# Rounding three output-projection weight chunks on GpSimd instead of ScalarE

## The reference

```python
hin = _rms_norm(x, norm_g[0])
z = hin @ w_in                                   # 1024 -> 2964, split into three head groups
y_moba = _moba_attention(...)                    # 4 heads x 64: top-3 past blocks of 256 keys + own block
y_ml = _mlstm_chunkwise(...)                     # 4 heads, qk 64, v 128, chunkwise matrix memory
y_nsa = _nsa_attention(...)                      # 4 query heads x 64: compressed + selected + window
y = concat([_head_norm(y_moba), _head_norm(y_ml) * sigmoid(lo), _head_norm(y_nsa)])
x = x + _rms_norm(y @ w_out, norm_g[1])          # the output projection, 1024 x 1024
hm = _rms_norm(x, norm_g[2])
y = square(relu(hm @ w1)) @ w2                   # MLP, hidden 4096
return x + _rms_norm(y, norm_g[3])
```

## Time and profile before

| | |
|---|---|
| time, median of 3 runs | 604.87 us (604.27 to 605.67) |
| the profiled execution | 604.64 us |
| its span in the trace | 602.9 us |
| busy in the span: TensorE | 593.0 us (98%) |
| VectorE | 387.6 us (64%) |
| ScalarE | 300.2 us (50%) |
| GpSimd | 256.5 us (43%) |
| attention in the trace | about 160 to 214 us |

### The profile page before, as it was taken

The page is one execution under the profiler, slowest core; times in us unless marked ns, Lnnn a source line. Parts: engine busy times, 40 slices in busy tenths (PEclk is TensorE's granted clock), DMA queues, the critical chain, the costliest instruction groups (busy, mean ns, idle before and its releaser), DMA issues.

```text
span 602.9 us, 8291 instructions
## 1 busy us (share of the span) xinstructions
PE 593.0 (98%) x3099; PEld 484.9 (80%) x3099; DVE 387.6 (64%) x665; ACT 300.2 (50%) x529; POOL 256.5 (43%) x137
## 2 busy tenths in 40 slices
PE   8999999999999999999999999999999999999995
PEld 5898888767867678899878888888888888888884
DVE  6414605265878773983999767585595685771657
ACT  7623414654589933555645536444345255454322
POOL 8563323573094610053357453631723626711611
PEclk9999999999999999999999999999999999999999
DMA  9743282365013820028034350621603404104002
GB/s 325 289 149 130 75 205 71 87 176 193 1 45 89 276 66 0 1 72 279 1 140 139 119 161 1 203 77 55 203 23 139 140 1 150 60 1 174 1 35 106
DMA packets 36580, 67.18 MB, mean 111 GB/s; under 512 B 2876, under 2 KB 23612, under 8 KB 35516
## 3 DMA queue, kind: packets, MB, share of 16 engines
q1 hardware_dynamic: 36236, 66.25, 34.1%
q10 hardware_dynamic: 304, 0.39, 0.3%
HBM read 62.18 MB, written 2.10 MB: 107 GB/s over the span
## 4 chain that ended last, share of the span: by engine, by line
PE 94%; ACT 2%; issue 2%; DVE 2%; POOL 0%; POOLq 0%; ACTq 0%; DVEq 0%
PE ps L1809 20%; PE ps L1811 20%; PE ps L1810 20%; PE ps L2283 7%; PE ps L2285 7%; PE ps L2284 7%; PE ps L2135 2%; PE ps L2150 2%; PE ps L2046 1%; PE ps L2047 1%; ACT probs L946 1%; PE ps L1975 1%; PE ps L2004 1%; PE ps L2211 1%; PE ps L2165 1%
## 5 line engine op out<-in xcount | busy, mean ns | idle before, releaser
L1809 PE MATMUL ps<-xT_h,ring_h 128*128 128x512 f32 (+1 forms) x384 | 144.7, 377 | 0.0
L1811 PE MATMUL ps<-xT_h,ring_l 128*128 128x512 f32 (+1 forms) x384 | 143.2, 373 | 0.0
L1810 PE MATMUL ps<-xT_l,ring_h 128*128 128x512 f32 (+1 forms) x384 | 143.1, 373 | 0.0
L770 POOL TENSOR_TENSOR ring_l<-raw_d,ring_h 128x1024 fp32r<-128x1024 f32 x25 | 67.3, 2697 | 129.8 <-ACT ring_h L1041 129.8
L770 POOL TENSOR_TENSOR ring_l<-raw,ring_h 128x1024 fp32r<-128x1024 f32 x31 | 76.7, 2499 | 77.5 <-DVE xres L1625 38.1
L694 POOL TENSOR_TENSOR ring_l<-raw,ring_h 128x512 fp32r<-128x512 f32 (+2 forms) x26 | 64.2, 2490 | 75.0 <-ACT ring_h L793 75.0
L1719 DVE TENSOR_TENSOR y<-ps,y 128x512 f32<-128x512 f32 x90 | 61.1, 688 | 51.0 <-PE ps L2285 50.7
L1809 PEld LDWEIGHTS ps<-xT_h,ring_h 128*128 128x128 f32 x384 | 72.4, 188 | 14.9 <-issue 2.4
L1811 PEld LDWEIGHTS ps<-xT_h,ring_l 128*128 128x128 f32 x384 | 72.3, 188 | 13.0
L1810 PEld LDWEIGHTS ps<-xT_l,ring_h 128*128 128x128 f32 x384 | 72.4, 189 | 12.4
L2283 PE MATMUL ps<-ring_h,a_h 128*128 128x512 f32 x196 | 76.7, 391 | 0.1
(11 more groups left out here) (277 smaller groups left out, 995.0 us busy)
## 6 DMA issues: line engine op xcount, KB each, us to landing
raw<-in_w_mlp SPq DMA_DIRECT2D x16, 1024.0 KB, 5.6
raw_d<-in_w_mlp SPq DMA_DIRECT2D x16, 1024.0 KB, 6.0
raw<-in_w_groups SPq DMA_DIRECT2D x8, 1024.0 KB, 4.8
xres<-in_x SPq DMA_DIRECT2D x8, 512.0 KB, 7.0
raw<-in_nsa_cmp_w SPq DMA_DIRECT2D x8, 512.0 KB, 6.4
raw<-in_w_groups SPq DMA_DIRECT2D x8, 256.0 KB, 5.3
raw<-in_w_out SPq DMA_DIRECT2D x2, 1024.0 KB, 5.1
raw<-in_w_out SPq DMA_DIRECT2D x4, 512.0 KB, 4.7
```

The costliest lines, as they stand in the source:

```text
L770: nc.gpsimd.tensor_tensor(slot(ring_l, n), slot_source(n), slot(ring_h, n).bitcast(F32), ALU.subtract).then_inc(lo_done, 1)
L1809: nc.tensor.matmul(o, sh, mh, start=start, stop=False)
L1810: nc.tensor.matmul(o, sh, ml, start=False, stop=False)
L1811: return nc.tensor.matmul(o, sl, mh, start=False, stop=stop)
```

## The change

In GpSimd's function a new helper makes both halves of a chunk, one directly behind the other; in ScalarE's loop the three calls go. The waits of `high_half` (the load has landed, the mLSTM outputs are done for the memory that they share, the earlier chunk in the same ring slot is used up) go with it to GpSimd.

```diff
-            low_half(C_WO + 1)
-            low_half(C_WO + 2)
-            low_half(C_WO + 3)
+            def both_halves(c):
+                pool.wait_ge(raw_in[c % RAW], raw_full(c))
+                if c >= C_WO + 2:
+                    pool.wait_ge(ml_o, 4)
+                if c < C_WO + 3:
+                    pool.wait_ge(*released(ring_previous(c)))
+                n, r = size(c), ring_slot(c)
+                for a in range(0, n, SEQ):
+                    last = nc.gpsimd.tensor_copy(ring_h[r][:, a:a + SEQ], raw[c % RAW][:, a:a + SEQ])
+                last.then_inc(hi_done, 1)
+                low_half(c)
+            for c in range(C_WO + 1, C_WO + 4):
+                both_halves(c)
...
-                if u == 11:
-                    high_half(C_WO + 1)
-                if u in (15, 19):
-                    high_half(C_WO + 2 + (u == 19))
```

## The result

The changed kernel takes 606.93 us (median of 8 runs, 606.34 to 607.28), the kernel before 605.00 us beside it: a ratio of 1.0033, 95% interval 1.0023 to 1.0042. It is slower by 0.33%, 1.93 us, inside the stated range and above the 605.7 us forecast. The profiled execution took 607.24 us with a span of 605.5 us.

What follows compares the result with a forecast made beforehand. TensorE, busy 98% of the span, was taken as the bound. 1.2 us lost to VectorE waiting for GpSimd, less 0.1 us won from ScalarE, is 1.1 us on 604.64: 605.7 us, range 604.3 to 607.2.

Steps and rivals of the forecast that it cites:

- What bounds the kernel: Whole kernel: TensorE, busy 98% of the span; in the changed stretch only 0.86 us of its idle time could be won.
- The chain of waits that ran through ScalarE: Third rounding in attention, from 202.34 us: as a rival, its 1.91 us go and the time is 602.7 us; chance 0.05.
- GpSimd's own work: Chunks 17 to 19: twelve copies of 0.62 us plus subtractions of 1.25 us, ending no later than before, 5 us to spare.
- the walk: Attention stretch: step-by-step timing of GpSimd's copies and subtractions against five VectorE operations; 1.2 us lost in all.
- The slow copy: GpSimd's copies as slow as two-input subtractions, so TensorE waits before the first projection product; 606.4 us, chance 0.07.
- The mechanism: Attention: a VectorE operation with two SBUF inputs waits until the GpSimd instruction under way is over, and TensorE waits behind it.
- the lock's cost: Attention: TensorE time lost to VectorE waiting for GpSimd at five places; 1.2 us, 0.6 to 2.4 by length of copy.
- the first four meetings: First four of five VectorE two-input operations that find GpSimd busy: 0.1, 0, 0 and 0.2 us lost; the fifth 0.9.
- The room: Slack before a late VectorE operation delays TensorE: 0.26, 0.42 and 0.24 us before values, 0.42 and 0.15 before transposes.
- the slow rival of the lock near half of its full price: Attention: VectorE's waits for GpSimd cost 2.4 us, half of a full 4.7; 607.0 us, chance 0.20.
- the 0.1 us of gain: Attention: what removing ScalarE's three roundings, 5.7 us of work, gives back; 0.1 us, bounds 0 and 0.86 us.
- slower by over 0.2%: Whole kernel: more than 1.2 us slower, chance 0.39; within 0.2% had 0.56, faster by over 0.2% had 0.05.

Runs made afterwards that it cites:

- write_only: Changed kernel, but GpSimd only writes zeros for both halves of chunks 17 to 19 and reads no SBUF; 604.82 us, ratio 0.9998.
- both_fixes: Changed kernel with line 1542's product kept in PSUM and line 1528 moved ahead of the copy of transposed probabilities; 604.08 us, ratio 0.9989.
- both_fixes_before: Kernel before, ScalarE's roundings kept, with the product kept in PSUM and the scale factors moved ahead of the copy of transposed probabilities; 604.39 us, ratio 0.9991.
- big_steps: Changed kernel with one GpSimd copy and one subtraction of 128x2048 a chunk in place of four of each; 614.88 us, ratio 1.0161.
- small_steps: Changed kernel with GpSimd copies and subtractions of 128x256, eight of each a chunk; 605.79 us, ratio 1.0016.

## Why the prediction came out as it did

- What bounds the kernel: right. The time grew by TensorE's idle time in the stretch (1.93 us between the medians, 1.96 us of idle time), and ScalarE's 5.7 us bought nothing that shows (write_only, and both_fixes against both_fixes_before). The chain of waits that ran through ScalarE was no price.
- GpSimd's own work: right. Copies were put at 0.62 us each and took 0.57 in a row (616 ns by the group's mean); GpSimd ended at 207.0 in a trace 0.6 us late, against the 208.4 of the walk. The slow copy and a wait ahead of the projection didn't occur.
- The mechanism: right. VectorE's two-input operations wait for GpSimd, and TensorE for them. Without GpSimd's reads the loss is gone (write_only), with long instructions it is 10 us, 7 of them TensorE's waits (big_steps), with VectorE's second input in PSUM line 1543 is free (both_fixes). One wait does not fit the rule that VectorE gets in when the GpSimd instruction under way is over: 1.2 us through some three copies (small_steps).
- The mis-sized term is the lock's cost: 1.2 us in the walk, 2.0 us measured (1.58 and 0.49 us of longer distances). The walk gave the first four meetings 0.3 us of loss together and the fifth 0.9. The run gave the second, third and fourth 0.62, 0.87 and 0.60 us of TensorE idle time and the first and fifth none. Two things were off in it.
  - The phase. The first line 1543, at 185.98, was not held, where the walk held it for 0.37 us, and each later meeting fell elsewhere. That the copies are shorter doesn't explain it: by the prediction's own steps copies of 0.58 us give 0.7 us, less than the walk and not more. The walk let VectorE in when a GpSimd instruction's row ends. By the rows of the run it gets in a little earlier: 0.15 us before the copies end at 185.98, and 0.12 us before a subtraction does at 195.07 (196.89 less its own 0.69 is 196.20; the subtraction ends at 196.32). So the subtractions came some 0.5 us sooner: the fourth began at 190.27 (191.52 less 1.25), less the 0.6 us by which this trace is late 189.67, against 190.15 in the walk. Line 1528 came just then and waited 1.06 us for it, where the walk had 0.4. The text had named this sensitivity, 0.6 to 2.4 us, and the measured value lies in it; which phase came is luck.
  - The room. The prediction took 0.42 and 0.15 us between VectorE's copy and TensorE's transposes. In the run TensorE starts 0.14 and 0.15 us after that copy has ended (192.94 and 202.93), with the copy the last step that it needs; that much is the hand-over, so the room was about 0.3 and 0. Ahead of the values the hand-over is 0.06 us. The measured delays (1.06, 1.13 and 0.48 us) less the prediction's rooms give 1.7 us: so the phase is some 0.5 us of the miss, the room some 0.3.
- The case that came is thus the slow rival of the lock near half of its full price, which had a chance of 0.20 (its 607.0 us leaves out the 0.1 us of gain that the other sums take off; with it 606.9); "slower by over 0.2%" had 0.39 and "within 0.2%" 0.56. The most likely class was wrong. The outcome of the walk hangs on a few hundredths of a microsecond of an operation that no row of the trace before shows. The five lengths of copy that it tried on its rows (1.2, 0.7, 0.6, 2.2 and 1.5 us) have a mean of 1.2 us, the bound itself, so slower and no change should have had about even chances.

## What to carry to other kernels

Before work moves to GpSimd, list VectorE's instructions with two SBUF inputs in that stretch and who waits for them: each can be held by GpSimd instructions that read SBUF, and the length of those instructions sets most of the price (614.88, 606.93 and 605.79 us with 2048, 512 and 256 elements). Putting one of the two inputs in PSUM, or moving the operation to where VectorE waits anyway, took the price away here and helped the kernel as it stood by 0.1%. Work taken off an engine that a saturated TensorE hides was worth nothing that could be measured, even though the chain of waits ran through it.

## What was not expected of the hardware

With copies of 0.35 us in a row, VectorE's sum waited 1.2 us, through some three of them, and got in only about where GpSimd paused for its own semaphore (small_steps). At other meetings it got in after one instruction. What decides that stays open. GpSimd's fills, which write SBUF and read none, held VectorE's two-input operations not at all (0.17 and 0.69 us in write_only). And where line 1543 was held for 4.2 us, TensorE lost more than its 3.95 us of idle time, since the values behind it ran 1.7 us longer, at a granted clock of 0.55 to 0.64 (big_steps).
